# Attention in three rounds a head instead of four, and head norms in batches of 3, 2 and 3

## The reference

```python
def diff_attention(h, k, v, rel_bias, w_q, q_norm, lq1, lk1, lq2, lk2, subln, w_o, lam_init):
    q = rms_norm((h @ w_q).reshape(bsz, seqlen, N_HEADS, 2, HEAD_DIM), q_norm)
    lam = exp(sum(lq1 * lk1)) - exp(sum(lq2 * lk2)) + lam_init
    def block(args):                       # 4 blocks of Q_BLOCK = 128 queries
        s = jnp.einsum("bqhcd,bkhcd->bhcqk", qc, k).astype(f32) * scale
        s = s + bias[None, :, None]
        s = jnp.where(rel <= 0, s, NEG_INF)
        pm = jax.nn.softmax(s, axis=-1)
        attn = pm[:, :, 0] - lam * pm[:, :, 1]
        return jnp.einsum("bhqk,bkhe->bqhe", attn.astype(v.dtype), v)
    o = rms_norm(o, subln) * (1.0 - lam_init)
    return o.reshape(bsz, seqlen, N_HEADS * 2 * HEAD_DIM) @ w_o
```

## Time and profile before

| | before |
|---|---|
| median of 3 runs | 2959.32 us (2958.28 to 2965.08) |
| profiled execution, its own time | 2957.08 us |
| its span | 2955.3 us |
| mean granted clock of PE | 0.971 |
| PE busy | 2630.2 us, 89% of the span |
| DVE busy | 1950.0 us, 66% |
| POOL busy | 1676.8 us, 57% |
| ACT busy | 827.5 us, 28% |
| attention rounds, first `highest` to the end of the last `values` | 2398.72 to 2504.10 us |

### The profile page before, as it was taken

One profiled execution on the slowest core, in us unless ns is written; L12 is line 12 of the kernel. 1 busy time (PEld: TensorE's weight loads), 2 busy tenths in 40 slices (PEclk: granted clock), 3 DMA queues, 4 the chain that ended last, 5 costly groups with the idle time before them and its releaser, 6 DMA issues.

```text
span 2955.3 us, 32422 instructions
## 1 busy us (share of the span) xinstructions
PE 2630.2 (89%) x9810; PEld 1213.2 (41%) x9810; DVE 1950.0 (66%) x3960; ACT 827.5 (28%) x1800; POOL 1676.8 (57%) x1024
## 2 busy tenths in 40 slices
PE   7989888888888788878878999999999988999999
PEld 3454333333333333333333774444444444444444
DVE  7947777777777777777878684566335685566523
ACT  2423222222222222222224562222122245222101
POOL 5544444444444444444444867777776641677776
PEclk9999999999999999999998979999999998999999
DMA  4259999999999999999961322233322310233322
GB/s 140 67 200 421 421 421 421 414 410 419 416 414 416 409 419 410 418 406 412 422 265 52 106 72 93 96 103 107 115 95 79 121 58 8 78 100 99 121 97 81
DMA packets 133100, 696.18 MB, mean 236 GB/s; under 512 B 29867, under 2 KB 31180, under 8 KB 67052
## 3 DMA queue, kind: packets, MB, share of 16 engines
q0 software_dynamic: 73728, 536.90, 44.1%
q1 hardware_dynamic: 59244, 157.74, 16.0%
HBM read 686.72 MB, written 7.86 MB: 235 GB/s over the span
## 4 chain that ended last, share of the span: by engine, by line
PE 31%; DMA 26%; POOLq 15%; DVE 13%; issue 8%; ACT 3%; DVEq 2%; POOL 2%; ACTq 0%; SPq 0%
DMA R<-expert_uv_dram,idx 26%; PE bank L558 19%; POOLq L2653 8%; PE bank L772 8%; POOLq L2651 7%; DVE R L2088 3%; POOL R L2678 1%; DVE Z L2110 1%; DVE xt L2372 1%; ACT Z L1374 1%; DVE R L1833 1%; PE bank L1128 1%; DVE R L2480 1%; PE bank L1103 0%; DVE ci L2034 0%
## 5 line engine op out<-in xcount | busy, mean ns | idle before, releaser
L772 PE MATMUL bank<-R,Z 128*128 128x512 f32 x2048 | 967.5, 617 | 232.1 <-ACT Z L1374 228.7
L2678 POOL DMA_INDIRECT R<-expert_uv_dram,idx x512 | 595.9, 1164 | 721.9 <-PE bank L772 669.6
L558 PE MATMUL bank<-R 128*128 128x512 f16 (+1 forms) x3936 | 866.0, 381 | 9.6 <-DVE R L1817 6.9
L2088 DVE SCALAR_TENSOR_TENSOR R<-R 128x1024 f32<-128x1024 f32 x512 | 623.0, 1222 | 201.8 <-DMA R<-expert_uv_dram,idx 200.6
L772 PEld LDWEIGHTS bank<-R,Z 128*128 128x128 f32 x2048 | 380.3, 194 | 803.5 <-issue 413.7
L2650 POOL TENSOR_TENSOR R<-wring,beat 128x1024 f16<-128x1024 f32 (+2 forms) x219 | 448.0, 2046 | 415.9 <-PE bank L558 369.2
L558 PEld LDWEIGHTS bank<-R 128*128 128x128 f16 (+1 forms) x3936 | 383.0, 98 | 491.2 <-issue 28.4
L2652 POOL TENSOR_TENSOR R<-wring,R 128x1024 bf16<-128x1024 f32 (+2 forms) x219 | 511.4, 2335 | 31.8 <-issue 0.3
L1374 ACT ACTIVATE Z<-consts,R 128x128 f32<-128x128 f32 x512 | 177.6, 394 | 321.5 <-DVE R L2100 321.2
L558 PE MATMUL bank<-Z,R 128*128 128x512 f16 x1104 | 239.9, 379 | 1.5 <-POOLq L2653 1.5
L1367 ACT ACTIVATE R<-R 128x2 f32<-128x2 f32 x256 | 52.1, 203 | 606.8 <-DVEq L2090 606.5
(11 more groups left out here) (365 smaller groups left out, 2537.0 us busy)
## 6 DMA issues: line engine op xcount, KB each, us to landing
wring<-up_dram SPq DMA_DIRECT2D x88, 512.0 KB, 3.5
wring<-down_dram SPq DMA_DIRECT2D x32, 704.0 KB, 4.1
wring<-ple_dram SPq DMA_DIRECT2D x16, 640.0 KB, 3.9
wring<-w_in_dram SPq DMA_DIRECT2D x18, 512.0 KB, 3.5
R<-expert_uv_dram,idx POOLq DMA_INDIRECT x512, 12.3
wring<-glu_dram SPq DMA_DIRECT2D x16, 512.0 KB, 4.0
Z<-w_q_dram SPq DMA_DIRECT2D x11, 512.0 KB, 7.8
wring<-ple_a_dram SPq DMA_DIRECT2D x8, 640.0 KB, 5.9
```

Source lines behind the costliest of these rows:

```text
L558: mm = pe.matmul(bank[:, :], low(w) if i else w, low(v) if j else v, start=(start and c == 0 and p == 0), stop=(stop and c == n - 1 and p ...
L772: mm = pe.matmul(banks[2 * par + c][:, :], diag[:, k % 4, :], pairs[:, slot, 1, c * SEQ:(c + 1) * SEQ], start=(k == 0), stop=(k == TOPK - 1))
L2088: dot = ve.scalar_tensor_tensor(pairs[:, slot, 0, :], pairs[:, slot, 0, :], 1.0, ntok[:, T, :], ALU.mult, ALU.mult, accum_out=act[:, par, ...
L2678: po.indirect_dma_start(pairs[:, slot, :, :].rearrange("p a b -> p (a b)"), None, A["expert_uv"], bass.IndirectOffsetOnAxis(idx[:, n % 2, ...
```

## The change

The 32 units become 24 rounds v: for each head one round for query blocks 0 and 1 together, one for block 2 and one for block 3 (`ROUNDS`). In the joint round both blocks' scores stand side by side in one pair of banks (columns 0 to 127 and 128 to 383), and the steps go over both (`members`); there is one `highest` drain, one `share` on two columns, one signal each way. `exps_until(v)` translates a round to the count of exponentials. The batches of norms become heads 0 to 2, 3 and 4, 5 to 7; SPREAD_AT, SPREADS_BEFORE and INVERSE_AT are given for rounds. The norm of head 5 moves behind the last `values`: with `first = HEADS - 3` the output product's first part takes five heads and the last part three, and three spreads stand between them. DVE makes the lower halves of heads 6 and 7 as before, with an additional wait for head 5's, which POOL makes.

```diff
-        BATCHES = ((0, 1, 2, 3), (4, 5), (6, 7))
+        ROUNDS = ((0, 1), (2,), (3,))
+        NR = len(ROUNDS)
+        BATCHES = ((0, 1, 2), (3, 4), (5, 6, 7))
         BATCH = [g for g in range(3) for h in BATCHES[g]]
-        SPREAD_AT = {21: 0, 22: 1, 23: 2, 25: 3, 27: 4, 29: 5}
-        SPREADS_BEFORE = {5: 3, 6: 5, 7: 6}
-        INVERSE_AT = {20: 0, 27: 1}
+        SPREAD_AT = {13: 0, 14: 1, 16: 2, 19: 3, 20: 4}
+        SPREADS_BEFORE = {4: 2, 5: 3, 6: 5, 7: 5}
+        INVERSE_AT = {12: 0, 18: 1}
...
+        def members(v):
+
+            at = 0
+            for part, qt in enumerate(ROUNDS[v % NR]):
+                w = (qt + 1) * P
+                yield part, v // NR * NT + qt, qt, at, w
+                at += w
+
+        def exps_until(v):
+
+            return 2 * (v // NR * NT + ROUNDS[v % NR][-1]) + 2
...
-                    if u >= 2:
-                        pe.wait_ge(exp_done, 2 * u - 2)
+                    if v >= 2:
+                        pe.wait_ge(exp_done, exps_until(v - 2))
...
-                first = HEADS - 2
+                first = HEADS - 3
...
                     if i == 1:
+                        spread(HEADS - 3, 6)
                         spread(HEADS - 2, 4)
                         spread(HEADS - 1, 5)
...
-                def share(u):
-                    b = u % 2
-                    ve.wait_ge(exp_done, 2 * u + 2)
-                    ve.reciprocal(ratio[:, b:b + 1], sums[:, u, 1:2])
+                def share(v):
+                    n, u = len(ROUNDS[v % NR]), v // NR * NT + ROUNDS[v % NR][0]
+                    r = ratio[:, v % 2, 0:n]
+                    ve.wait_ge(exp_done, exps_until(v))
+                    ve.reciprocal(r, sums[:, u:u + n, 1])
                     ve.drain()
...
+                head_norm(HEADS - 3, 6)
                 head_norm(HEADS - 2, 4)
                 head_norm(HEADS - 1, 5)
                 for h in (HEADS - 2, HEADS - 1):
                     ve.wait_ge(on_hi, h + 1)
+                    ve.wait_ge(x_split, KT * SPLITS.index("attn") + HEADS - 2)
```

More of the change, by code:

```diff
@@ L1096, in scores2 @@
                         pe.wait_ge(gq_sqrt, 2 * HEADS)
-                    if u >= 2:
-                        pe.wait_ge(exp_done, 2 * u - 2)
-                    if u == 3:
+                    if v >= 2:
+                        pe.wait_ge(exp_done, exps_until(v - 2))
+                    if v == 3:
                         pe.wait_ge(evac_done, used(TILE0["w_v"] + 7))
[L1101 to L1104, removed]
@@ L1105, in scores2 @@
-                    mm.then_inc(at_sc, 1)
[L1107 to L1117, removed]
+                    for part, u, qt, at, w in members(v):
+                        for c in range(2):
+                            rows, out = slice(c * HD, (c + 1) * HD), banks[score_bank(v) + c]
+                            mm = pe.matmul(out[:, at:at + w], KQ[rows, HEADS + h, qt * P:(qt + 1) * P], KQ[rows, h, 0:w],
+                                           start=True, stop=True)
@@ L1197, in _ @@
                 for i in range(3):
-                    out_product(i, n=2, ready=x_split if i == 0 else None, base=base + first, start=False,
-                                first_of_slab=(i > 0), order=(first, first + 1)).then_inc(mm_done, 1)
+                    out_product(i, n=HEADS - first, ready=x_split if i == 0 else None, base=base + first, start=False,
+                                first_of_slab=(i > 0), order=range(first, HEADS)).then_inc(mm_done, 1)
                 for i in range(3, SLABS["attn_o"]):
@@ L2565, in _ @@
                 ve.drain()
[L2567 to L2577, removed]
-                        ve.tensor_tensor_reduce(both[:, c, w - near:w], both[:, c, w - near:w],
-                                                near_bias[:, u // NT, 2 * P - near:], 1.0,
-                                                far_min[:, b, c:c + 1] if w > near else -NEG, ALU.add, ALU.min,
-                                                nm[:, b, c:c + 1])
-                    ve.drain().then_inc(mx_ready, 1)
@@ L2584, in share, with highest @@
[L2584 to L2587 removed]
+                def highest(v):
+                    b = v % 2
+                    ve.wait_ge(at_sc, v + 1)
+                    if v >= 2:
+                        ve.wait_ge(exp_done, exps_until(v - 2))
+                    both = psum[:, score_bank(v) * SEQ:(score_bank(v) + 2) * SEQ].rearrange("p (c k) -> p c k", k=SEQ)
+                    for part, u, qt, at, w in members(v):
+                        near = min(w, 2 * P)
+                        if w > near:
+                            ve.tensor_reduce(far_min[:, b, :], both[:, :, 0:w - near], AX, ALU.min)
+                            ve.drain()
+                        for c in range(2):
+                            ve.tensor_tensor_reduce(both[:, c, at + w - near:at + w], both[:, c, at + w - near:at + w],
+                                                    near_bias[:, v // NR, 2 * P - near:], 1.0,
+                                                    far_min[:, b, c:c + 1] if w > near else -NEG, ALU.add, ALU.min,
+                                                    nm[:, b, part, c:c + 1])
+                    ve.drain().then_inc(mx_ready, 1)
@@ L2728, in beside_attention @@
                         po.drain().then_inc(split_done, 1)
-                    for h in range(4):
+                    for h in range(5):
                         if h == 1:
```

92 lines of the change are left out of this document (52 added, 40 removed).

## The result

| | before | after |
|---|---|---|
| median | 2959.32 us (2955.51 to 2965.08, 5 runs) | 2942.66 us (2941.35 to 2947.84, 5 runs) |
| profiled execution | 2957.08 us | 2942.78 us |
| its span | 2955.3 us | 2941.0 us |

The ratio after to before is 0.9948, with a 95% interval of 0.9937 to 0.9959: 15.4 us less, between 12.1 and 18.6 (the medians themselves differ by 16.7). I had forecast 9.5 us less, 2949.8, and a range down to 2944.5.

A forecast was written before the change was run, and what follows sets the result against it. DVE's queue was taken to bound the clean heads. The terms -5.2 - 1.0 + 1.3 - 5.2 - 0.9 + 1.0 - 0.6 gave -10.6, less 1.1 for semaphore steps: -9.5 us, median 2949.8, range 2944.5 to 2957.5.

The forecast's parts named there:

- start of the rounds: Before the first `highest` of head 0: nothing there depends on the changed code except where two rounds' scores are issued; 0.
- share and drain, 8 heads: DVE in each head: one share and one drain removed, 0.65 us a head; -5.2 us, ends 0 and 5.2.
- head 0 beside this: Head 0: `blend(0)` no longer held by POOL's subtraction, against later value copies; -1.0 us, between 0 and -2.
- POOL beside the rounds, heads 1 to 3: POOL in all heads: 1.78 us hold stays; +0.5 for the third split, +0.8 for five `norm_low` steps.
- waits and holds in heads 4 to 7: DVE's waiting around two root sequences and head 7: 9.1 us against 14.3; -5.2 us, ends -1 to -8.
- norm of head 5 off DVE: DVE queue in the loop: head 5's norm leaves it for behind the last `values`; -0.9 us.
- tail: Last blend to end of the last `values`: 5.6 us instead of 6.2; -0.6 us.
- behind the last `values`: PE after the last `values`: head 5's eight spread products are added there; +1.0 us.
- rival (b): Heads: joint round leaves ACT or PE no cover, or DVE waits as long in heads 5 to 7; 2955.5, chance 0.18.
- rival (a): Tail: falls to the lower clock, both last `values` take 4.0 to 4.6 us, some +3.5; 2953, chance 0.2.
- The warning I had given for myself: Sign of a wrong forecast, on PE: `values` waiting for norms for more than 1 us.
- The two waits of 2 to 3 us for scores: Sign of a right forecast: DVE waits twice for scores, in heads 5 and 6, 2 to 3 us each.

The follow-up runs named there:

- The later split: Kernel before with POOL's second and third slab split beside the rounds waiting for two exponentials more; 2956.89 us against 2957.81, ratio 0.9992.
- new batches: Kernel before, still 32 units, with the change's norm batches and head 5's norm behind the last `values`; 2951.73 us against 2957.81, ratio 0.9979.
- fillers before: Kernel before with three unused fp32 products on PE in each gap behind a root; 2954.68 us against 2957.81, ratio 0.9987.
- the second timing: Changed kernel timed once more, unaltered; 2943.15 us against 2957.44 for the kernel before, ratio 0.9952.
- single shares: Changed kernel with separate reciprocals, products and drains per block of the joint round and a drain inside its `highest`; 2949.38 us, ratio 0.9965 to the kernel before.
- the longer root: Changed kernel with four small square roots and drains on ACT ahead of the first and second root; 2946.43 us against 2943.15 for the change.

## Why the prediction was right or wrong

| step | predicted | in the two profiled executions |
|---|---|---|
| start of the rounds | 0 | +0.9 |
| share and drain, 8 heads | -5.2 | -6.0 |
| head 0 beside this | -1.0 | -1.05 |
| POOL beside the rounds, heads 1 to 3 | +1.3 (all heads) | -2.4 |
| waits and holds in heads 4 to 7 | -5.2 | -8.2 |
| norm of head 5 off DVE | -0.9 | -0.9 |
| tail | -0.6 | +1.5 |
| behind the last `values` | +1.0 | +1.9 |
| sum | -10.6, less 1.1: -9.5 | -14.3 |

**What bounds a head** was right: DVE's queue. 9.18 became 8.43 us, and undoing the merging on DVE alone brought 9.18 back. The term was mis-sized by 0.1 us a head: I counted 0.12 us for the drain, from the end of the accumulator's reading, but without a drain the next step starts with that reading, so a drain is worth 0.26 us. 0.26 + 0.53 is 0.79, of which 0.75 shows. In heads 1 to 3 after the change DVE never waited for ACT or PE; rival (b) is out.

**Start.** I noted that the first two rounds' scores are issued inside the value product and gave it no cost. PE spends 1.57 us there instead of 0.93, and the value product ends 0.64 us later. The rest of the 0.9 is the spread between executions.

**POOL.** This step failed, in sign too (+1.3 forecast). I wrote that the splits "stay where they were in terms of heads" and that the hold of 1.78 us "stays". I had read the split's length and the share's length and not who wakes both. They hang on the same exponential, so the joint round's order decides the overlap. Heads 0 to 3 are 40.66 us in the earlier trace rows, head 0 alone 10.23 by the trace, so heads 1 to 3 take 30.43, where three clean heads of 9.18 would be 27.54: 2.9 us of holds and waits. Two held shares of head 2 are 2.2 of them: 1.78 and, one unit later, 0.86 us, where the step takes 0.22. After, heads 1 to 3 take 25.74, and three of 8.43 are 25.29: 0.45 us. Only one share is held there, for 0.66 us. The later split takes 1.8 us of the holds out of head 2 by itself. The extra +0.5 and +0.8 us were not there either: in heads 4 to 7 the steps held beside POOL are 1.3 us too long in the profile before and 1.3 in the one after.

**Waits in heads 4 to 7.** The mechanism (root, gap, lower clock, slow `values`, DVE waits for scores) is real: fillers that close the gaps took 6.1 us out of heads 5 to 7 in the trace of the kernel before, and 4.6 us out of the median of the changed kernel. The step that failed is its carrying over: I let the clock fall behind both roots for certain, and at 2.6 and 2.7 us of wait for scores each. In the first execution of the change it fell behind neither, in the second behind one; where it fell, the wait was 0.4 to 1.9 us. The profile after shows where the 3 us between 5.2 and 8.2 went. DVE's waits in heads 4 to 7 are 4.1 us in all, where I had counted 9.1. For the scores it waits 1.20 us, not 5.3. For the spreads it waits 0.92 and 1.25 us, as I had counted (1.05 each). The small waits come to 0.7 us, not 1.7. Before, the same waits were 12.2 us; my 14.3 had been got by subtraction and also held the 1.3 us of steps held beside POOL and some 0.8 us besides. The waits thus fell by 8.1 us, which is the row's whole 8.2.

**Tail.** The order was as I walked it, and at the full clock it takes 6.01 us (5.6 predicted; the terms of that chain add up to 8.55 us and not 8.8, so by my own terms it would have been 5.35). In the first execution `values(6)` ran at the lower clock behind its wait for the norm of head 4 and it was 7.70. That is half of rival (a), whose price of 3.5 us counted both `values`. The warning I had given for myself, `values` waiting for norms for more than 1 us, came true (1.87 us) without spoiling the rest.

**Behind the last `values`.** The 8 additional products take 0.9 us on PE (24 take 2.94 us, 16 took 2.05), near the 1.0 predicted. But the kernel before spent the first microsecond of this part at the lower clock, which the change does not, and with the clock up throughout this part takes 451.4 us with 24 products, against its 451.2. The clock that falls behind the 24 is the rest, 1.6 to 1.7 us, and was in no term of the sum.

**The signs.** Of those I had named, the clean head near 8.5 us (8.43), the 24 reciprocals, the absence of a 4 us wait before the last share and the 24 spread products behind the last `values` came true. The two waits of 2 to 3 us for scores did not: there was one, of 1.20 us. And from the first `highest` to the last `values`' end it took 88.3 us, not 95.

**What no row of before could show** is that its own profile was a favourable execution. The kernels with four units and untouched heads 1 to 3 (new batches, fillers before) had them at 32.9 us instead of 30.4: their clock stayed at the lower level longer (0.65 in head 1, against 0.79), and behind the POOL hold it fell again (0.86 in head 2, against 1.00; with the later split it stayed at 1.00 there too). All the executions with joint rounds and merged shares have 25.7 us there, whether the clock in head 1 is 0.90 or 0.71. This may be part of why the medians of the first timing differ by more than the profiled executions (16.7 us against 14.3); in the second timing they differ by 14.3 as well, and it was not measured by itself.

**The balance.** The change is worth 14 to 17 us in two timings. The new batches alone are 6.1 of them. Joint rounds without the merging on DVE bring 2.4 more, with most of the POOL hold (2 us by the trace, not shown by time) and of head 0 in it. Merged shares and drains are 6.0 by the trace of the clean heads and 4 to 8 by undoing them. The terms overlap where the clock is concerned, so their sum isn't the whole to a microsecond.

## What to carry to other kernels

When an engine waits for its own queue, count what a merged step saves from start to start of its neighbours in the trace, drain included, and not from ends to starts. Where two engines share a port and hang on the same semaphore, their collision is part of the program: look for who wakes both, and move one of them by one step. Don't carry a fall of PE's clock from one schedule to another as a certainty: give it as a probability with the wait that a trace shows behind it, and if the gaps sit in known places, close them with products that nobody uses; here that brought another 3 to 5 us for some ten lines of code.

## What the runs showed of the hardware

The length of a gap on PE did not decide whether its clock fell. Behind the first root a gap of 2.88 us left it up in two executions of the change and brought it down with single shares. Behind the second a gap of 2.69 us left it up in one execution of the change and brought it down in the next. The gap ahead of `values(4)`, 0.94 us, was followed by a fall in both (`values(4)` took 4.1 us); with the longer root a gap of 0.93 us at that place was not (2.39 us). The longest gaps, 3.96 and 3.77 us, both brought it down, and so did those of 2.73 to 3.27 us in head 0 in all twelve profiled executions (the scores behind them took 2.1 us where the same form takes 1.13). What else decides was not found out. The Trainium skill (TensorE: Matmul & The Clock Gate, The HAM clock gate) says that the activity window runs freely and doesn't start with the kernel; the two executions of one program, with the same gaps and different falls, agree with that.

The clock also fell with no gap, behind 24 products whose weights have only 16 rows (0.61 and 0.54 in the two stretches from 2498 to 2502 us) in five executions of seven, and not behind 16 of them in any of five. Whether it is their small use of the array or their number was not tried.

A hold between POOL and DVE was the same to 0.01 us in three kernels that share the trigger (1.78 us), so it can be planned for.
